# Router products one projection behind their transposes, and the first expert's bias rows asked for before the meeting

## The chip, the cores and the metric

The kernel runs on one core of one Trainium2 chip. The metric is the device time of one execution in microseconds (us). The core has five engines that run their own instruction streams side by side and meet through semaphores: TensorE (PE in the profile), VectorE (DVE), ScalarE (ACT), GpSimd (POOL) and SyncE (SP, which here only asks for transfers). Sixteen DMA engines move data.

## The reference, cut to what matters

One transformer block with a mixture of experts, then a second model of two layers. The change lies in the first block, between the output projection of the mixer and the first expert:

```python
x = x + gate1 * (mixed @ w_out)                      # 512 rows x 1024
h = rmsnorm(x, norm2_w) * (1.0 + scale2) + shift2
logits = h @ w_router + b_router                     # 512 x 32
top_val, top_idx = lax.top_k(logits, 4)
gates = softmax(top_val)
# rows are sorted by expert into blocks of up to 128
hu = xb @ w_up[e] + b_up[e]                          # for each block
act = x_glu * sigmoid(1.702 * x_glu) * (x_lin + 1)
y = act @ w_down[e] + b_down[e]
```

All of this is computed in float32; the bias rows are added as three bfloat16 parts, in a product with ones.

## The kernel before

The kernel is one program in stages. Each stage has one function for each engine (`pe_out1`, `dve_out1`, `act_out1`, `pool_out1` for the router stage; `pe_experts` and so on for the experts), and the code's order in it is the order of that engine's instructions. `meet` joins the engines between stages: each drains and counts up its `finished` semaphore, and each waits for all of them. GpSimd doesn't drain at the meeting ahead of the experts (`but=nc.gpsimd`), but waits for the others.

**Router stage.** The 512 rows are four tiles of 128. `pe_project` (L1286 on) multiplies the mixer's output by `w_out` in two halves of 512 columns (c = 0, 1), each for four tiles: 8 products of 128x512 in float32 make one projection of a tile and a half. In the second half it calls `between(i)` behind tile i's projection. In the kernel before this is `logits(i - 1)`: 4 + 4 transposes of the normed rows of tile i-1 into two PSUM banks (`h2t`, L223), then the product with the router weight, 8 products of 128x32 (L217). The product waits until both banks have been copied into `H2T`: one by VectorE (`features`, L1367), one by ScalarE (L1504). Behind the loop stands `logits(3)`.

VectorE, in `dve_project`, takes each projection out of its bank, multiplies it by the gate (L1308), adds it to x (L1311), and then calls its own `between(i)`: copy half of turned tile i-1 (`features`), make the normed rows of tile i (`h2_rows`, L1356 to L1363, with the sum of squares and the root from ScalarE, L1499 and L1501), and add the bias to the logits of tile i-1 and select its four experts (`logits`, L1371 to L1385, ten small operations in a chain). Behind the loop: `features(3)`, `logits(3)`, and then some 90 small operations that rank the experts and build the row lists.

Each product takes the next of eight PSUM banks in turn (`next_bank`), and waits until the engine that reads that bank has emptied it.

**Meeting and experts.** GpSimd waits for the row lists, gathers the rows of the first two blocks (`pool_gather`, L1682), and waits at the meeting. Then `pool_experts` asks for the bias rows of eight experts (`pool_biases`, L1689), of which the first is always expert 0, in a place known when the kernel is built. TensorE turns the first block's rows (L223), and `pe_up` begins with four products of the bias rows and ones (L1589), which wait for that transfer, before it multiplies by the weights (L1601; L1630 in `pe_down`). Weight tiles of 2 MB come through seven slots; SyncE asks for the next one when TensorE has read the slot's last tile. The expert loads beyond the first expert need VectorE's list of places.

The bias rows of the experts land in `BU`, whose memory the router stage uses for other tiles.

Of the kernel before, what the change touches and what calls it, by code (L numbers as in the profile page):

```python
# [26 lines left out]
NBU = 8  # L27
# [68 lines left out]
def emit(nc, D, out, ctx):  # L96
# [53 lines left out]
    BIASD = dram("bias_rows", (NEXP, 3, 3072), BF16)  # L150
# [9 lines left out]
    done, bank, read = {}, {}, {}  # L160
# [41 lines left out]
    def next_bank(e, key):  # L202
        turn[0] = (turn[0] + 1) % len(order)
        return fill(e, order[turn[0]], key)
# [338 lines left out]
    MIX = alloc(8, 512)  # L543
# [742 lines left out]
    def pe_project(e, src, tcs, tag, between=None):  # L1286

        for c in range(2):
            m, w = take()
            w = x512(w)  # L1290
            e.wait_ge(*landed[m])
            for i in tcs:
                o = next_bank(e, (tag, c, i))
                products(e, o, [(src[:, k, i * 128:i * 128 + 128], w[:, k, :]) for k in range(8)]).then_inc(*pe.up())
                done[tag, c, i] = pe.now()
                if c and between:
                    between(i)
            used[m] = pe.now()
# [15 lines left out]
                    between(i)  # L1314

    def pe_out1(e):
        def logits(i):
            for g in range(2):
                o = next_bank(e, ("h2t", i, g))
                e.wait_ge(*signal("h2_made").at(i + 1))  # L1320
                transposes(e, [(o[:, q * 128:q * 128 + 128], H2[:, i, (4 * g + q) * 128:(4 * g + q + 1) * 128]) for q in range(4)]).then_inc(*pe.up())
                done["h2t", i, g] = pe.now()
            o = next_bank(e, ("logit", i))
            for g in range(2):
                e.wait_ge(*emptied(("h2t", i, g)))
            if i == 0:
                e.wait_ge(*dr.at(96))
            products(e, o[:, 0:32], [(H2T[:, k, i * 128:i * 128 + 128], wr[:, k, :]) for k in range(8)]).then_inc(*pe.up())
            done["logit", i] = pe.now()

        pe_project(e, MIX, range(4), "out1", lambda i: logits(i - 1) if i else None)
        logits(3)
        for l in range(2):
            o = next_bank(e, ("later", l))
            e.wait_ge(*dvr[l].at(16))
            transposes(e, [(o[:, 0:48], vrows2[0:48, l, :])]).then_inc(*pe.up())
            done["later", l] = pe.now()
        o = next_bank(e, "ranks")
        e.wait_ge(*signal("masks").at(1))
        products(e, o[:, 0:128], [(ones, BF[:, 0:4, :]), (U_, MM)])  # L1340
        products(e, o[:, 128:160], [(ones, BF[:, 4, :])]).then_inc(*pe.up())
        done["ranks"] = pe.now()
        o = next_bank(e, "rows")
        for n in range(16):
            u = n % 4
            e.wait_ge(*signal("picks").at(n + 1))
            e.matmul(o[:, 0:NBLK], OP[:, u, :], OBK[:, u, 0:NBLK], start=(n == 0), stop=(n == 15)).then_inc(*pe.up())
            done["pick", n] = pe.now()

    def dve_out1(e):  # L1350
# [14 lines left out]
        def features(i):  # L1365
            e.wait_ge(*done["h2t", i, 0])
            e.tensor_copy(H2T[:, 0:4, i * 128:i * 128 + 128], bank["h2t", i, 0].rearrange("p (k n) -> p k n", n=128)).then_inc(*empties(("h2t", i, 0)))  # L1367
# [28 lines left out]
        def between(i):  # L1396

            if i:
                features(i - 1)
            h2_rows(i)  # L1400
            if i:
                logits(i - 1)

        e.memset(BF[:, 0, :], 0.0).then_inc(*dve.up())
        e.wait_ge(*dr.at(96))
# [1 line left out]
        e.wait_ge(*dg.at(16))  # L1407
        e.wait_ge(*dxa.at(16))
        dve_project(e, range(4), "out1", lambda i: X[:, i, :], lambda i: GR, TM, between)
        features(3)  # L1410
        logits(3)
        for l in range(2):
# [117 lines left out]
    act_out1(nc.scalar)  # L1530
    pool_out1(nc.gpsimd)
    load_on(nc.sync, n_exp + NSLOT)
    row_lists, mix_read = done["row_lists"], done["out1", 1, 3]


    top[0] = base
# [158 lines left out]
    main = Lane("a")  # L1695
# [105 lines left out]
    def pool_experts(e):  # L1801
        places = {}

        def biases(x):
            p = sequence[x]
            xr = in_place(e, places, p)
            rows = BIASD[bass.ds(xr, 1)].rearrange("a k n -> (a k) n") if p else BIASD[0]
            pool_biases(e, main, x, rows, last_block[sequence[x - NBU]] if x >= NBU else None)

        def store(i):  # L1810
            if i < NMAIN - 1:
                pool_store(e, main, i, blocks[i].col)
            for x in range(NBU, NEXP):
                if last_block[sequence[x - NBU]] == i:
                    biases(x)

        for x in range(NBU):
            biases(x)
        for i in range(NMAIN):
            if i + 2 < NMAIN:  # L1820
                pool_gather(e, main, i + 2, blocks[i + 2].col)
            if i and not blocks[i - 1].again:
                store(i - 1)
            if blocks[i].again or i == NMAIN - 1:
                store(i)
# [4 lines left out]
        nc.gpsimd.wait_ge(*t)  # L1830
    for i in range(2):
        pool_gather(nc.gpsimd, main, i, blocks[i].col)
    meet([dz.now()], but=nc.gpsimd)
    next_stage()
    pe_experts(nc.tensor)
# [1061 lines left out]
```

## Time and profile before

| | us |
|---|---|
| median of 3 runs | 2846.61 |
| lowest and highest | 2844.38, 2846.85 |
| the profiled execution | 2849.81 |
| its span in the profile | 2848.6 |
| TensorE busy in it | 2587.0 (91%) |
| VectorE busy | 997.6 (35%) |
| ScalarE busy | 563.5 (20%) |
| GpSimd busy | 170.6 (6%) |
| second half of the output projection to the first expert's start | 573 to 669 |
| expert stage | 669 to 1814 |

Times in the profile are microseconds from the start of the span. The timeline merges like instructions that follow each other; the bracket at the end of a row is the idle time of that engine ahead of it and what ended it. A float32 product is recorded as two instructions, so a projection of 8 products is x16. The granted clock is a share of TensorE's 2.4 GHz; 0.50 is its lower level, 1.2 GHz.

### The profile page before, as it was taken

What the parts mean: (1) busy time and instruction counts of PE and PEld (TensorE: products, weight loads), DVE (VectorE), ACT (ScalarE), POOL (GpSimd) and SP (SyncE); (2) the same over time, 40 slices, a digit from 0 to 9 for tenths busy, and PEclk for the clock granted to TensorE, in tenths of its full rate; (3) what the DMA queues carried; (4) which work ended last, traced back from release to release, by engine and by line L of the source; (5) the groups of instructions that cost most, each with busy time, mean ns of one, the idle gap of its engine ahead of it and who ended that gap; (6) DMA issues with size and microseconds to landing.
All of it is one profiled execution on the core that took longest, in us unless ns stands there. A gap on an engine that the chain in (4) does not pass through costs nothing. (4 is left out here: it accounts for less than half of the span.)

```text
span 2848.6 us, 27020 instructions
## 1 busy us (share of the span) xinstructions
PE 2587.0 (91%) x10285; PEld 1257.0 (44%) x10285; DVE 997.6 (35%) x2141; ACT 563.5 (20%) x1274; POOL 170.6 (6%) x316
## 2 busy tenths in 40 slices
PE   5979788876999999999999999798999889999998
PEld 2534556343434333443443333465544444454453
DVE  2665344353112111111121111435176665332272
ACT  1354313010000000000000000211255443200250
POOL 0000414101000000000000000200000000000000
PEclk8998999987999999999999999899989899999889
DMA  9110175716999999958959999710000002112000
GB/s 327 64 59 30 60 293 166 297 59 260 389 400 416 409 410 415 416 217 338 356 200 370 411 418 416 288 59 26 30 1 1 1 1 82 40 64 89 30 1 30
DMA packets 143354, 565.43 MB, mean 198 GB/s; under 512 B 15429, under 2 KB 36158, under 8 KB 105202
## 3 DMA queue, kind: packets, MB, share of 16 engines
q1 hardware_dynamic: 127336, 515.97, 46.2%
q0 software_dynamic: 12992, 42.51, 4.0%
q10 hardware_dynamic: 2890, 5.13, 0.5%
q8 instruction: 85, 1.39, 0.2%
q14 instruction: 51, 0.42, 0.0%
HBM read 537.24 MB, written 26.35 MB: 198 GB/s over the span
## 5 line engine op out<-in xcount | busy, mean ns | idle before, releaser
L1601 PE MATMUL ps<-ring,mem 128*32 128x512 f32 (+2 forms) x1888 | 517.6, 602 | 8.4 <-issue 8.4
L217 PE MATMUL ps<-mem,ring 128*128 128x512 f32 (+1 forms) x1056 | 421.8, 559 | 2.6 <-DVE mem L737 1.6
L217 PE MATMUL ps<-ring,mem 128*128 128x512 f32 (+5 forms) x1136 | 397.0, 507 | 29.4 <-DVEq L182 15.0
L1601 PEld LDWEIGHTS ps<-ring,mem 128*32 128x32 f32 (+2 forms) x1888 | 189.4, 146 | 276.5 <-issue 276.5
L217 PEld LDWEIGHTS ps<-mem,ring 128*128 128x128 f32 x1056 | 201.5, 192 | 213.2 <-issue 204.6
L217 PEld LDWEIGHTS ps<-ring,mem 128*128 128x128 f32 x1136 | 202.4, 197 | 210.1 <-issue 178.3
L1630 PE MATMUL ps<-ring,mem 128*32 128x512 f32 (+2 forms) x1056 | 273.5, 618 | 11.0 <-issue 11.0
L223 PE MATMUL ps<-mem 128*128 128x128 f32 (+3 forms) x1203 | 195.3, 296 | 70.9 <-DVEq L182 19.8
L1601 PE MATMUL ps<-mem 128*32 128x512 f32 (+2 forms) x800 | 235.0, 596 | 0.0
L223 PEld LDWEIGHTS ps<-mem 128*128 128x128 f32 (+3 forms) x1203 | 146.9, 148 | 195.0 <-issue 126.4
L1662 DVE COPY mem<-ps 128x512 f32<-128x512 f32 x48 | 33.3, 693 | 521.5 <-PE ps L223 521.5
L1670 ACT ACTIVATE mem<-mem 128x512 f32<-128x512 f32 x48 | 28.1, 632 | 771.6 <-DVE mem L1646 771.6
L1638 DVE COPY mem<-ps 128x512 f32<-128x512 f32 x48 | 33.3, 693 | 400.8 <-PE ps L223 400.8
L1630 PEld LDWEIGHTS ps<-ring,mem 128*32 128x32 f32 (+2 forms) x1056 | 100.3, 143 | 161.6 <-issue 161.6
L2350 PE MATMUL ps<-ring 64*128 64x256 f32 (+4 forms) x328 | 132.3, 526 | 14.0 <-ACT mem L2455 4.2
L2405 DVE TENSOR_REDUCE mem<-ps 128x1 f32<-128x768 f32 (+3 forms) x128 | 99.1, 774 | 129.9 <-PE ps L2350 123.0
L1601 PEld LDWEIGHTS ps<-mem 128*32 128x32 f32 (+2 forms) x800 | 83.6, 145 | 107.1 <-issue 107.1
L1630 PE MATMUL ps<-mem 128*128 128x512 f32 (+2 forms) x288 | 119.6, 595 | 0.5 <-issue 0.5
L2465 ACT ACTIVATE ring<-ps 128x768 f32<-128x768 f32 (+2 forms) x128 | 75.5, 603 | 120.9 <-PE ps L223 120.7
L2118 ACT ACTIVATE mem<-ps 128x512 f32<-128x512 f32 (+2 forms) x68 | 33.1, 488 | 331.0 <-PE ps L217 331.0
L2350 PEld LDWEIGHTS ps<-ring 64*128 64x128 f32 (+1 forms) x328 | 62.3, 213 | 62.9 <-issue 49.6
L1677 ACT ACTIVATE mem<-ps 128x512 f32<-128x512 f32 x48 | 26.1, 596 | 310.6 <-PE ps L1630 310.6
(376 smaller groups left out, 2366.7 us busy)
## 6 DMA issues: line engine op xcount, KB each, us to landing
ring<-in_w_up SPq DMA_DIRECT2D x91, 2048.0 KB, 15.7
ring<-in_w_down SPq DMA_DIRECT2D x47, 2048.0 KB, 21.6
mem<-in_w_up SPq DMA_DIRECT2D x37, 2048.0 KB, 19.2
mem<-in_w_down SPq DMA_DIRECT2D x17, 2048.0 KB, 20.7
ring<-in_w_ada SPq DMA_DIRECT2D x12, 2048.0 KB, 7.5
ring<-in_mod_w SPq DMA_DIRECT2D x8, 2048.0 KB, 10.2
ring<-in_cd_w_in SPq DMA_DIRECT2D x6, 2048.0 KB, 7.7
y_rows<-mem POOLq DMA_DIRECT2D x23, 512.0 KB, 8.2
```

What stands on the lines that cost most here:

```text
L217: i = e.matmul(o, l, r, start=(n == 0), stop=(n == len(pairs) - 1))
L223: r = e.transpose(o, i, ident[0:k, 0:k])
L1601: m = e.matmul(PS[n][c0:c0 + rows, :], XGT[:, u, k * 128 + c0:k * 128 + c0 + rows], wt[:, kk, n * 512:n * 512 + 512], start=False, stop=(k ...
L1630: m = e.matmul(PS[6 + n][c0:c0 + rows, :], ACTT[:, k * 128 + c0:k * 128 + c0 + rows], wt[:, kk, n * 512:n * 512 + 512], start=False, stop= ...
L1638: e.tensor_copy(XGT[:, i % 2, hh * 512:hh * 512 + 512], PS[4]).then_inc(L.x_copied, 1)
L1662: e.tensor_copy(ACTT[:, hh * 512:hh * 512 + 512], PS[5]).then_inc(L.a_copied, 1)
L1670: e.activation(SG[:, c], T1[:, c], ACT.Sigmoid, scale=1.702).then_inc(L.gate, 1)
L1677: e.activation(Y[:, i % 2, n * 512:n * 512 + 512], PS[6 + n], ACT.Copy).then_inc(L.y_copied, 1)
L2118: e.activation(dst, bank[key][:, 0:n], func).then_inc(*empties(key))
L2350: m = e.matmul(PP[x % 2][:, at:at + k.shape[1]], q, k, start=True, stop=True)
L2405: e.tensor_reduce(m[:, 0:1], PP[x % 2][:, lo:lo + n], AX.X, ALU.max).then_inc(*dve.up())
L2465: m = e.activation(A.groups[g][1][a][:, to:to + k1 - k0, c * 128:c * 128 + 128], PP[2][:, k0 * 128:k1 * 128].rearrange("p (k n) -> p k n", ...
```

## The change

Router stage, TensorE: the function `logits` is split. `turn_h2(i)` does the transposes of tile i, `logits(i)` the product. Behind the projection of tile i TensorE now does `turn_h2(i - 1)` and then `logits(i - 2)`; behind the loop `logits(2)`, `turn_h2(3)`, `logits(3)`. VectorE's `between(i)` keeps the copy of turned tile i-1 and the normed rows of tile i, and selects for tile i-2 rather than i-1; behind the loop it selects for tile 2, copies turned tile 3, and selects for tile 3. ScalarE's code is the same.

Meeting: GpSimd asks for expert 0's bias rows behind the two gathers and ahead of the meeting. A wait stands in front of it, for the product of tile 3, since the rows go to memory that the router's products read. `pool_experts` begins with the second expert of its sequence.

```diff
--- before.py
+++ after.py
@@ -1314,12 +1314,14 @@
                     between(i)
 
     def pe_out1(e):
-        def logits(i):
+        def turn_h2(i):
             for g in range(2):
                 o = next_bank(e, ("h2t", i, g))
                 e.wait_ge(*signal("h2_made").at(i + 1))
                 transposes(e, [(o[:, q * 128:q * 128 + 128], H2[:, i, (4 * g + q) * 128:(4 * g + q + 1) * 128]) for q in range(4)]).then_inc(*pe.up())
                 done["h2t", i, g] = pe.now()
+
+        def logits(i):
             o = next_bank(e, ("logit", i))
             for g in range(2):
                 e.wait_ge(*emptied(("h2t", i, g)))
@@ -1328,7 +1330,16 @@
             products(e, o[:, 0:32], [(H2T[:, k, i * 128:i * 128 + 128], wr[:, k, :]) for k in range(8)]).then_inc(*pe.up())
             done["logit", i] = pe.now()
 
-        pe_project(e, MIX, range(4), "out1", lambda i: logits(i - 1) if i else None)
+        def between(i):
+
+            if i:
+                turn_h2(i - 1)
+            if i > 1:
+                logits(i - 2)
+
+        pe_project(e, MIX, range(4), "out1", between)
+        logits(2)
+        turn_h2(3)
         logits(3)
         for l in range(2):
             o = next_bank(e, ("later", l))
@@ -1398,8 +1409,8 @@
             if i:
                 features(i - 1)
             h2_rows(i)
-            if i:
-                logits(i - 1)
+            if i > 1:
+                logits(i - 2)
 
         e.memset(BF[:, 0, :], 0.0).then_inc(*dve.up())
         e.wait_ge(*dr.at(96))
@@ -1407,6 +1418,7 @@
         e.wait_ge(*dg.at(16))
         e.wait_ge(*dxa.at(16))
         dve_project(e, range(4), "out1", lambda i: X[:, i, :], lambda i: GR, TM, between)
+        logits(2)
         features(3)
         logits(3)
         for l in range(2):
@@ -1530,7 +1542,7 @@
     act_out1(nc.scalar)
     pool_out1(nc.gpsimd)
     load_on(nc.sync, n_exp + NSLOT)
-    row_lists, mix_read = done["row_lists"], done["out1", 1, 3]
+    row_lists, mix_read, features_read = done["row_lists"], done["out1", 1, 3], done["logit", 3]
 
 
     top[0] = base
@@ -1814,7 +1826,7 @@
                 if last_block[sequence[x - NBU]] == i:
                     biases(x)
 
-        for x in range(NBU):
+        for x in range(1, NBU):
             biases(x)
         for i in range(NMAIN):
             if i + 2 < NMAIN:
@@ -1830,6 +1842,9 @@
         nc.gpsimd.wait_ge(*t)
     for i in range(2):
         pool_gather(nc.gpsimd, main, i, blocks[i].col)
+    assert sequence[0] == 0
+    nc.gpsimd.wait_ge(*features_read)
+    pool_biases(nc.gpsimd, main, 0, BIASD[0], None)
     meet([dz.now()], but=nc.gpsimd)
     next_stage()
     pe_experts(nc.tensor)
```

TensorE's order in the second half of the output projection, before. x48 is the first half and two tiles of the second; L223 x8 are the transposes of a tile; 128x32 are the router's products.

```order
L217 MATMUL ps<-ring,mem 128x512 x48
L223 MATMUL ps<-mem 128x128 x8
L217 MATMUL ps<-mem 128x32 x8
L217 MATMUL ps<-ring,mem 128x512 x8
L223 MATMUL ps<-mem 128x128 x8
L217 MATMUL ps<-mem 128x32 x8
L217 MATMUL ps<-ring,mem 128x512 x8
L223 MATMUL ps<-mem 128x128 x8
L217 MATMUL ps<-mem 128x32 x8
L223 MATMUL ps<-mem 128x128 x8
L217 MATMUL ps<-mem 128x32 x8
```

The same place on TensorE with the change:

```order
L217 MATMUL ps<-ring,mem 128x512 x48
L223 MATMUL ps<-mem 128x128 x8
L217 MATMUL ps<-ring,mem 128x512 x8
L223 MATMUL ps<-mem 128x128 x8
L217 MATMUL ps<-mem 128x32 x8
L217 MATMUL ps<-ring,mem 128x512 x8
L223 MATMUL ps<-mem 128x128 x8
L217 MATMUL ps<-mem 128x32 x16
L223 MATMUL ps<-mem 128x128 x8
L217 MATMUL ps<-mem 128x32 x8
```

The products of tiles 0 and 1 stand one projection later, the one of tile 1 now behind the last projection, in a row with that of tile 2.

GpSimd around the meeting, before, with the semaphores that each instruction waits for. L1682 are the gathers, L1689 the bias rows, L380 reads an expert's number; the `finished` semaphores are the meeting.

```order
L1524 DMA h_rows<-mem 128x1024 [waits h2_made] x4
L1682 DMA mem<-h_rows,mem 128x1024 [waits dma_h2,bank_free1,pe_step]
L1682 DMA mem<-h_rows,mem 128x1024
L1689 DMA mem<-bias_rows 3x3072 [waits pool_finished,act_finished,dma_zero,dve_finished,pe_finished]
L380 TENSOR_LOAD mem [waits dve_step]
L380 ISA x2
L1689 ISA
L1689 DMA mem<-bias_rows 3x3072
```

The same place on GpSimd with the change (`pe_step` on the bias rows is the product of tile 3):

```order
L1536 DMA h_rows<-mem 128x1024 [waits h2_made] x4
L1694 DMA mem<-h_rows,mem 128x1024 [waits dma_h2,bank_free1,pe_step]
L1694 DMA mem<-h_rows,mem 128x1024
L1701 DMA mem<-bias_rows 3x3072 [waits pe_step]
L380 TENSOR_LOAD mem [waits pool_finished,dma_zero,act_finished,dve_step,dve_finished,pe_finished]
L380 ISA x2
L1701 ISA
L1701 DMA mem<-bias_rows 3x3072
```

The first request for bias rows has left the meeting's waits to the instruction behind it.

## Rows read from the trace of the kernel before

**Rows 1.** Timeline, TensorE, router and first expert (start, us, engine line operation, idle before)
```profile
587.51 1.04 PE L223 MATMUL ps<-mem 128*128 128x128 f32 x8
591.48 1.94 PE L217 MATMUL ps<-mem 128*128 128x32 f32 x16 [2.93 <-ACT mem L1504]
593.26 8.81 PE L217 MATMUL ps<-ring,mem 128*128 128x512 f32 x16
...
605.82 2.38 PE L217 MATMUL ps<-mem 128*128 128x32 f32 x16 [2.88 <-ACT mem L1504]
608.02 8.37 PE L217 MATMUL ps<-ring,mem 128*128 128x512 f32 x16
616.22 1.04 PE L223 MATMUL ps<-mem 128*128 128x128 f32 x8
620.14 2.99 PE L217 MATMUL ps<-mem 128*128 128x32 f32 x16 [2.88 <-ACT mem L1504]
...
626.54 3.59 PE L217 MATMUL ps<-mem 128*128 128x32 f32 x16 [1.66 <-DVE mem L1367]
...
661.96 1.09 PE L223 MATMUL ps<-mem 128*128 128x128 f32 x4 [7.21 <-DVEq L182]
664.02 1.09 PE L223 MATMUL ps<-mem 128*128 128x128 f32 x4 [0.97 <-DVE mem L1638]
669.22 1.88 PE L1589 MATMUL ps<-mem 3*128 3x512 bf16 x4 [4.11 <-DMA mem<-bias_rows]
```

**Rows 2.** Timeline, VectorE, router
```profile
592.29 1.23 DVE L1363 TENSOR_TENSOR mem<-mem 128x1024 f32<-128x1024 f32 x1
...
621.05 1.23 DVE L1363 TENSOR_TENSOR mem<-mem 128x1024 f32<-128x1024 f32 x1
623.16 0.19 DVE L1371 TENSOR_TENSOR mem<-ps,mem 128x32 f32<-128x32 f32 x1 [0.88 <-PE ps L217]
...
625.75 0.69 DVE L1367 COPY mem<-ps 128x512 f32<-128x512 f32 x1
630.17 0.19 DVE L1371 TENSOR_TENSOR mem<-ps,mem 128x32 f32<-128x32 f32 x1 [3.73 <-PE ps L217]
```

**Rows 3.** Timeline, GpSimd, second gather and first request for bias rows
```profile
657.59 0.97 POOL L1682 DMA_INDIRECT mem<-h_rows,mem  x1 [0.31 <-issue]
662.42 0.58 POOL L1689 DMA_DIRECT2D mem<-bias_rows  x1 [3.86 <-DVE mem L1491]
```

**Rows 4.** Timeline, TensorE, transposes and projections in a later stage
```profile
2454.23 1.04 PE L223 MATMUL ps<-mem,ring 128*128 128x128 f32 x8
2455.10 7.03 PE L217 MATMUL ps<-ring,mem 128*128 128x512 f32 x16
```

**Rows 5.** Windows: length, busy time (instructions) of PE, PEld, DVE, ACT, POOL, clock, DMA share, GB/s
```profile
593.00:596.00 3.00, 3.00 (x8) 1.46 (x8) 2.72 (x14) 0.00 (x0) 0.54 (x1) 0.58 0.37 150
...
626.00:629.00 3.00, 2.46 (x12) 2.48 (x12) 0.44 (x1) 0.82 (x1) 0.00 (x0) 0.50 0.01 3
671.00:674.00 3.00, 3.00 (x5) 1.42 (x5) 0.00 (x0) 0.00 (x0) 1.30 (x2) 0.50 1.02 405
674.00:677.00 3.00, 3.00 (x6) 1.19 (x6) 0.00 (x0) 0.00 (x0) 0.00 (x0) 0.76 1.01 386
710.00:713.00 3.00, 3.00 (x18) 1.00 (x16) 0.00 (x0) 0.00 (x0) 0.00 (x0) 1.00 0.02 5
```

**Rows 6.** DMA: second gather, first bias request (us to landing), all bias-row transfers
```profile
mem<-h_rows,mem POOLq DMA_INDIRECT x1, 4.9
...
mem<-bias_rows POOLq DMA_DIRECT2D x1, 18.0 KB, 6.7
...
DMA to landing us min/median/max: 2.5/7.8/10.0
```

**Rows 7.** Waits of TensorE, expert stage, 660 to 1760 us (in total, times, longest)
```profile
PE ps L1601 <- issue: 8.4, 5, 3.6
...
PE ps L1630 <- issue: 3.9, 2, 3.1
```


## The prediction

> **What bounds the kernel now.** I read the waits of the router stage first, then its TensorE and VectorE timelines, then the windows of the expert stage. The question is not which engine is busiest over 2848.6 us, but which wait ends last in the two places that the change touches, and whether what is won there arrives at the end.
>
> *Router.* In the second half of the output projection TensorE does, for each tile i after the first: project tile i, turn the normed rows of tile i-1 (8 transposes), multiply them by the router weight. The product needs both copies of the turned tile out of PSUM, so TensorE stands still behind the transposes: 2.93 us before the product of tile 0, and 2.88 before that of tile 1 [rows 1]. The third such gap, before the product of tile 2, comes after the last projection. From the last projection on VectorE leads: it makes the normed rows of tile 3, selects for tile 2, copies half of turned tile 3, waits for the product of tile 3, selects for tile 3 (630.17), and goes on in one chain of small dependent operations to 661.8, which releases TensorE at 661.96 [rows 1, 2]. So the stage ends when tile 3's logits exist plus a constant, and those hang on when the last projection ends.
>
> *Meeting.* TensorE turns the first block's rows and is ready at 664.02 + 1.09 = 665.11. It starts the first expert at 669.22, after 4.11 us of waiting for the bias rows, which GpSimd asks for at 662.42, just behind the meeting [rows 1, 3].
>
> **Part 1, projections ahead of products.** The transposes of tile i-1 are now followed at once by projection i+1, and the product of i-1 stands one projection later. I build TensorE's new order from starts. The same alternation of 8 transposes and a projection runs elsewhere at the full clock: 0.87 us from the start of the transposes to that of the projection, which is recorded at 7.03 [rows 4] and overlaps what follows by some 0.16 (608.02 + 8.37 is 0.17 past 616.22, [rows 1]), so 6.87 to the next transposes. The product takes 593.26 - 591.48 = 1.78 from start to start [rows 1].
> - Turn tile 0 at 587.51 (unchanged), projection 2 at 588.38, turn tile 1 at 595.25, product 0 at 596.12, projection 3 at 597.90, turn tile 2 at 604.77. Before, turn tile 2 began at 616.22 [rows 1]. So it is **11.45 us** earlier: two gaps of 2.93 and 2.88; the product of tile 1, 608.02 - 605.82 = 2.20, now behind; two projections at 7.03 in place of 8.81 and 8.37, that is 3.12; and 0.3 of overlap.
> - The 3.12 need an argument. Projection 2 ran with a granted clock of 0.58 in 593 to 596, between the levels 1.2 and 2.4 GHz, though its predecessor ran full: the clock fell after 5.7 us in which TensorE had only transposes, a gap and the short product [rows 1, 5]. With the gap filled the clock should hold, as it does in the alternation of rows 4; the difference is the product of 32 columns that now stands beside the transposes.
> - Is the input ready? Turn tile 1 needs the normed rows of tile 1, whose last step ends at 592.29 + 1.23 = 593.52 [rows 2]: 1.7 us before 595.25. Product 0's copies (late by 2.9 us behind the transposes before) have a whole projection to finish in. PSUM banks rotate over eight and the order of TensorE's takes and of the copies leaves none late.
>
> **Part 1, what stands behind the last projection.** Before, VectorE's normed rows of tile 3 were ready at 621.05 + 1.23 = 622.28 [rows 2], 6.06 us after the start of turn tile 2 (616.22). That delay is VectorE's and ScalarE's own and stays: 604.77 + 6.06 = 610.83. Behind it VectorE now has two selections, of tiles 1 and 2, where it had one. One takes 625.75 - 623.16 = 2.59 [rows 2]. So 610.83 + 2 x 2.59 = 616.01 for the start of the copy of half of turned tile 3; from that copy to the product 626.54 - 625.75 = 0.79, and from the product to the selection of tile 3 630.17 - 626.54 = 3.63 [rows 1, 2]: 616.01 + 0.79 + 3.63 = 620.43 against 630.17. **The router is 9.7 us shorter**; 1.7 of the 11.45 go to the second selection (2.59, less the 0.88 that VectorE used to wait for product 2). TensorE fits in beside it: product 2 came 3.92 us after the start of turn tile 2 (620.14), so now at about 608.7, and tile 3 is turned by 613, with 3 us to spare.
>
> The 3.63 are a product at the low level, clock 0.50 in 626 to 629 [rows 5]. TensorE again has 3 us idle ahead of it, so I keep them. At the full level it would be 1.94, as product 0 [rows 1]: at best 1.7 more.
>
> All that follows (the chain of VectorE, the lists, the meeting, the first load of a chosen expert, which waits for VectorE's list) moves with 630.17, so these 9.7 us arrive whole.
>
> **Part 2, the bias rows.** GpSimd asks for expert 0's rows right behind its two gathers. Its new wait, for the product of tile 3, was met some 30 us earlier, and nothing queues behind it that it could hold. The second gather is issued at 657.59 for 0.97 us [rows 3], so the request goes out near 658.7 (in the old time) rather than 662.42, 3.7 us earlier. It landed 6.7 us after issue [rows 6]: 665.4. TensorE starts at 665.4 instead of 669.22: **3.8 us**. Bounds: all 4.1 if it lands before 665.1. At the other end its slowest landing of the whole trace, 10.0 us [rows 6], gives 668.7 and 0.5. I take 6.7, measured for this very request with three large transfers beside it; the gather's 4.9 [rows 6] means that the queue ahead is empty at 662.5, so nothing long is in the way. GpSimd's other bias requests follow the meeting in the old order, one place sooner.
>
> The Trainium skill, "DMA: Bandwidth & Descriptors", section "Queues, rings and completion order", says that a completion lands only after every earlier write of the same DMA engine, over all queues. By that rule the request now has only the gathers ahead of it and not the weight and context loads of 660 to 663, and the 6.7 would shrink; landing near 663, it would give 4.1 and a sum 0.3 larger. No row of before shows the request in that place.
>
> **Does the stage of the experts keep it?** It could be that the weight stream sets its pace. In 660 to 1760 TensorE waits 8.4 + 3.9 us for transfers [rows 7], so the stream is near its limit. But in 710 to 713 the DMA engines are 0.02 busy [rows 5]: they have caught up and wait for TensorE to free a slot, so the stream restarts from TensorE's time and takes its shift along. Before that, loads are asked for well ahead of their use. I take nothing off.
>
> **Sum.** 9.7 + 3.8 = 13.5 us. The profiled execution took 2849.81 us and would take 2836.3; the median of the runs is 3.2 lower, 2846.61, and would become **2833.1 us**, 0.47% less.
>
> **Rivals.**
> - *The clock falls in projections 2 and 3 all the same.* Speaks for it: turn and product together are 3 us of light work, and the clock fell after such work before, with a gap in it. Against: rows 4, and no gap remains. Price: the 3.12, so 10.4 us and 2836.2. The Trainium skill, "TensorE: Matmul & The Clock Gate", section "What's actually happening", puts the clock down to a monitor of recent activity that runs free of the kernel; by it the moment of a fall is partly luck, which lends this rival its chance.
> - *The bias rows bring little.* The small request lands late (10.0 us), or the load stream beside it takes back what TensorE wins: the slots of expert 0 come free earlier while the engines are 1.02 busy in 671 to 674 [rows 5]. Then only the router counts, 9.7 to 10.2 us: 2836.7. The change then does half of what it says.
> - *More than forecast.* The clock, low until about 675 [rows 5], rises sooner because TensorE is busy without a gap from 661.96: half of the 4.1 us moved, 2.0; product 3 at the full level, 1.7; bias 4.1. Sum 17.5, 2829.1.
> - *Slower: the weight stream slips.* Place: the waits of the expert products for landed tiles [rows 7]. An earlier TensorE meets the stream where it cannot follow, and each wait is followed by a stretch at the low clock: from 671 to 675 such a stretch cost about 2 us. If seven waits double (12.3 us) and each brings one more such stretch (up to 14), 26 us come against 13.5: 2846.6 - 13.5 + 26 = 2859. It decides from 13.5 us given back, and shows as slower from 19.2. Half of it, 7.8 to 19.2, would show as no change. Against: the idle DMA engines at 710, from which both start together.
>
> **How the numbers follow.** Forecast (2831.5 to 2835) 60 in 100; clock falls 13; bias brings little 11; more than forecast 7; stream slips 9, of which 6 end within 0.2% and 3 slower. Within 0.2% (5.7 us, about what a measurement of this kernel can tell from no change): 6; faster by more: 91; slower: 3. The range leaves out the stream rival and runs from 2829.1, less 1 us for the runs, to 2839.8, where the clock falls and the bias brings 0.5 (9.7 - 3.1 + 0.5 = 7.1, so 2839.5): 2828 to 2840.
>
> **What would show it.** Right: no gap between the transposes and projection 2 or 3, both at 7.0 us; from the start of turn tile 0 to that of turn tile 2 17.3 us; from there to the selection of tile 3 15.7 us (13.95 before); bias rows asked for within 0.5 us of the second gather, and under 0.5 us of wait before the first expert; waits for tiles in the expert stage near 12 us in sum. Wrong: projections over 8 us; a wait of 2 us or more for the bias rows; a stage of experts, from its first bias product to the start of the next stage, longer by some us than before.

## The result, and the profile after

| | before | changed |
|---|---|---|
| median, 6 runs each (us) | 2847.22 | 2833.23 |
| lowest, highest | 2844.38, 2856.25 | 2827.69, 2836.06 |
| the profiled execution | 2849.81 | 2832.91 |
| its span | 2848.6 | 2831.7 |

The ratio is 0.9941, with a 95% interval from 0.9924 to 0.9959: 0.4 to 0.8% faster. The medians differ by 14.0 us and the profiled executions by 16.9.

TensorE in the router stage of the changed kernel, and up to the first expert (the timeline: start, us, engine, line, operation, idle time before it and what ended it). It answers to [rows 1]:

```profile
587.69 1.04 PE L223 MATMUL ps<-mem 128*128 128x128 f32 x8
588.57 7.03 PE L217 MATMUL ps<-ring,mem 128*128 128x512 f32 x16
595.43 1.04 PE L223 MATMUL ps<-mem 128*128 128x128 f32 x8
596.31 1.87 PE L217 MATMUL ps<-mem 128*128 128x32 f32 x16
598.01 7.11 PE L217 MATMUL ps<-ring,mem 128*128 128x512 f32 x16
604.96 1.04 PE L223 MATMUL ps<-mem 128*128 128x128 f32 x8
...
608.88 1.94 PE L217 MATMUL ps<-mem 128*128 128x32 f32 x16 [1.17 <-ACT mem L1516]
...
616.90 3.60 PE L217 MATMUL ps<-mem 128*128 128x32 f32 x16 [3.80 <-DVE mem L1378]
...
652.33 1.09 PE L223 MATMUL ps<-mem 128*128 128x128 f32 x4 [7.21 <-DVEq L182]
654.39 1.08 PE L223 MATMUL ps<-mem 128*128 128x128 f32 x4 [0.98 <-DVE mem L1650]
655.40 1.88 PE L1601 MATMUL ps<-mem 3*128 3x512 bf16 x4
657.22 23.22 PE L1613 MATMUL ps<-ring,mem 128*128 128x512 f32 x48
```

No row from 587.69 to 604.96 has a bracket: both gaps of 2.9 us are gone, and both projections take 7.0 to 7.1 us where they took 8.81 and 8.37. The bias product at 655.40 has no bracket either; it waited 4.11 us before. The wait that grew is the one ahead of the product of tile 3, 3.80 us (1.66 before).

VectorE behind the last projection, for [rows 2]: the end of the normed rows of tile 3, the selections of tiles 1 and 2, the copy of half of turned tile 3, the selection of tile 3.

```profile
609.79 1.23 DVE L1374 TENSOR_TENSOR mem<-mem 128x1024 f32<-128x1024 f32 x1
610.93 0.18 DVE L1382 TENSOR_TENSOR mem<-ps,mem 128x32 f32<-128x32 f32 x1
...
613.52 0.19 DVE L1382 TENSOR_TENSOR mem<-ps,mem 128x32 f32<-128x32 f32 x1
...
616.11 0.69 DVE L1378 COPY mem<-ps 128x512 f32<-128x512 f32 x1
620.54 0.19 DVE L1382 TENSOR_TENSOR mem<-ps,mem 128x32 f32<-128x32 f32 x1 [3.73 <-PE ps L217]
```

GpSimd at the meeting, for [rows 3]. The first request for bias rows goes out with the second gather, the next one behind the meeting:

```profile
647.95 0.97 POOL L1694 DMA_INDIRECT mem<-h_rows,mem  x1 [0.31 <-issue]
648.92 0.60 POOL L1701 DMA_DIRECT2D mem<-bias_rows  x1
653.83 0.55 POOL L1701 DMA_DIRECT2D mem<-bias_rows  x1 [4.31 <-issue]
```

Windows of the changed kernel (length, busy times and counts of PE, PEld, DVE, ACT, POOL, then granted clock, DMA share, GB/s), for [rows 5]. The clock stays at 1.00 through the router's projections and falls behind the last one:

```profile
593.00:596.00 3.00, 3.00 (x13) 1.51 (x12) 1.06 (x2) 0.00 (x0) 0.54 (x1) 1.00 0.29 117
...
605.00:608.00 3.00, 2.71 (x25) 2.59 (x23) 2.13 (x4) 1.15 (x2) 0.00 (x0) 1.00 0.00 0
611.00:614.00 3.00, 1.94 (x8) 1.57 (x8) 2.62 (x17) 0.84 (x2) 0.53 (x1) 0.50 0.43 175
```

TensorE's waits for transfers from 660 to 1760 us, for [rows 7]: 14.4 us in sum, 12.3 before. These fixed limits cut the two executions at different places, since the changed one is 14 us ahead at their far end. Counted over the whole stage, from the first bias product to the stage behind the experts, the waits are 11.6 + 8.4 = 20.0 us before and 11.4 + 9.6 = 21.0 in the changed kernel.

```profile
PE ps L1613 <- issue: 9.6, 6, 3.3
...
PE ps L1642 <- issue: 4.8, 3, 3.2
```

The stage behind the experts starts with this row (14.01 us earlier than before, where it is 1814.39):

```profile
1800.38 1.94 PE L223 MATMUL ps<-mem 128*128 128x128 f32 x8 [10.14 <-PEq L1950]
```

### The profile page after: what moved, and what is told of

Same layout as the page of the kernel before. It is cut to its first block and busy times, and to the rows that moved or that the text cites. A ratio compares the mean times of both kernels' runs of the same rounds, so it can differ in the third digit from the quotient of the medians.

```text
span 2831.7 us, 27022 instructions
## 1 busy us (share of the span) xinstructions
PE 2577.2 (91%) x10285; PEld 1254.2 (44%) x10285; DVE 997.4 (35%) x2141; ACT 563.0 (20%) x1274; POOL 170.3 (6%) x316
## 5 line engine op out<-in xcount | busy, mean ns | idle before, releaser
L217 PE MATMUL ps<-ring,mem 128*128 128x512 f32 (+5 forms) x1136 | 390.8, 501 | 29.9 <-DVEq L182 15.0
L1642 PE MATMUL ps<-ring,mem 128*32 128x512 f32 (+2 forms) x1056 | 268.0, 598 | 11.4 <-issue 11.4
L223 PE MATMUL ps<-mem 128*128 128x128 f32 (+3 forms) x1203 | 195.6, 297 | 72.5 <-DVEq L182 19.9
L223 PEld LDWEIGHTS ps<-mem 128*128 128x128 f32 (+3 forms) x1203 | 147.0, 149 | 196.7 <-issue 129.1
L1682 ACT ACTIVATE mem<-mem 128x512 f32<-128x512 f32 x48 | 28.1, 632 | 771.9 <-DVE mem L1658 771.9
L1689 ACT ACTIVATE mem<-ps 128x512 f32<-128x512 f32 x48 | 26.1, 596 | 305.0 <-PE ps L1642 305.0
```

What stands on the lines that cost most here:

```text
L217: i = e.matmul(o, l, r, start=(n == 0), stop=(n == len(pairs) - 1))
L223: r = e.transpose(o, i, ident[0:k, 0:k])
L1642: m = e.matmul(PS[6 + n][c0:c0 + rows, :], ACTT[:, k * 128 + c0:k * 128 + c0 + rows], wt[:, kk, n * 512:n * 512 + 512], start=False, stop= ...
L1682: e.activation(SG[:, c], T1[:, c], ACT.Sigmoid, scale=1.702).then_inc(L.gate, 1)
```

## The experiments

Executions reach the router up to 7 us apart, and the later stages differ from one execution to the next by more than the change is worth (below). So the traces are compared by stretches between fixed places. A is from the turn of tile 0 on TensorE to the selection of tile 3 on VectorE. B is from there to the first bias product. C is from there to the first transposes of the stage behind the experts. All are differences of starts in the timelines, in us.

| kernel | A | B | C | ratio to before, interval |
|---|---|---|---|---|
| before | 42.66 | 39.05 | 1145.2 | |
| changed | 32.85 | 34.86 | 1145.0 | 0.9941, 0.9924 to 0.9959 |
| e1_router | 32.85 | 38.98 | 1146.4 | 0.9969, 0.9952 to 0.9985 |
| e2_bias | 42.66 | 34.88 | 1145.9 | 0.9990, 0.9978 to 1.0002 |
| e3_fill | 39.08 | 38.34 | 1145.4 | 0.9989, 0.9972 to 1.0006 |
| e4_tail | 30.34 | 34.88 | 1143.1 | 0.9937, 0.9915 to 0.9959 |
| e5_warm | 32.85 | 33.96 | 1145.7 | 0.9958, 0.9944 to 0.9971 |
| e6_after | 32.85 | 34.88 | 1145.2 | 0.9951, 0.9937 to 0.9966 |
| e7_both | 30.33 | 34.19 | 1145.1 | 0.9933, 0.9919 to 0.9946 |
| e8_mark | 32.85 | 34.89 | 1146.7 | |
| e9_hold | 29.02 | 34.87 | 1145.4 | 0.9933, 0.9915 to 0.9951 |
| e10_all | 29.02 | 33.68 | 1142.1 | 0.9930, 0.9913 to 0.9947 |
| e11_tail2 | 30.33 | 34.86 | 1143.9 | 0.9947, 0.9931 to 0.9963 |

A repeats within 0.03 us for the same code, and so does B in the kernels that ask early for the bias rows (34.86 to 34.89), so a tenth of a microsecond in these can be read. B is less certain where its end is a wait for the bias rows: from the selection of tile 3 on, the kernel before, e1_router and e3_fill have the same code, and B is 39.05, 38.98 and 38.34. Absolute starts that an expectation names hold for a router that starts as in the kernel before; the differences are what can be compared.

**One part alone: e1_router and e2_bias.** Against the changed kernel, e1_router asks for the bias rows where the kernel before did:

```diff
-    nc.gpsimd.wait_ge(*features_read)
-    pool_biases(nc.gpsimd, main, 0, BIASD[0], None)
     meet([dz.now()], but=nc.gpsimd)
...
-        for x in range(1, NBU):
+        for x in range(NBU):
```

e2_bias is the kernel before with these lines the other way round.

> Only part 1: the products one projection behind their transposes; GpSimd asks for the first bias rows behind the meeting, as in the kernel before. My theory: the selection of tile 3 starts 9.7 us earlier than in the kernel before (630.17 us of its span becomes 620.5), TensorE still waits about 4.1 us for the bias rows, and the first bias product starts at 659.4 instead of 669.22; the next stage (first transposes at 1814.4 before) starts at 1804.7; the whole is 9.7 us shorter, ratio 0.9966. Rival (the two parts are not additive, since an earlier meeting changes what stands beside the bias transfer): the bias wait is above 5 or under 3 us, and the gain at the first expert is off 9.7 by the same. Second rival (the weight stream takes gains back): the gain at the start of the next stage is smaller than at the first expert by 2 us or more.

> Only part 2: the first bias rows asked for ahead of the meeting; the router stage as before. The trace of the changed kernel showed no wait at all for the bias rows. My theory: the wait of 4.11 us before the first bias product goes and nothing takes its place, so that product starts at 665.1 instead of 669.22, and the stage behind the experts starts 4.1 us earlier (1810.3); ratio 0.9986. Rival (the weight stream takes it back, because the loads of chosen experts are asked for at the same time as before and TensorE only reaches them sooner): the gain at the start of the next stage is under 2 us and the waits of the expert products for transfers, 12.3 us before, grow by the rest. This is the sharper place to see it than the whole change, since here TensorE moves and the start of the stream does not.

e1_router, the first expert on TensorE:

```profile
663.28 1.88 PE L1601 MATMUL ps<-mem 3*128 3x512 bf16 x4 [4.03 <-DMA mem<-bias_rows]
```

e2_bias, the same place:

```profile
661.75 1.09 PE L223 MATMUL ps<-mem 128*128 128x128 f32 x4 [0.97 <-DVE mem L1638]
662.77 1.88 PE L1589 MATMUL ps<-mem 3*128 3x512 bf16 x4
```

Part 1 alone takes 9.81 us off A and leaves B; part 2 alone leaves A and takes 4.17 off B. The wait of 4.03 us is there with part 1 alone, so an earlier meeting hardly changes it; in e3_fill below, where only the router's order of work differs, it is 3.40, so the wait itself varies by some 0.7 us. The parts add: 9.81 + 4.19 in the changed kernel. Against the B of e3_fill, part 2 would be worth 3.5. C changes by +1.2, +0.7 and -0.2 us in the three; the same code gives 1145.0 and 1145.2 in two executions, 1143.1 and 1143.9 in two others (e4_tail, e11_tail2), and e8_mark, whose instructions before the experts differ only on GpSimd, 1146.7. No loss of 2 us or more in the weight stream shows; one of up to some 1.5 us cannot be told from that scatter. The waits for transfers over the whole stage are 19.9 us in e2_bias against 20.0 before, so they did not take back what part 2 won. By whole times e1_router's ratio is clear of 1 and fits 0.9966; e2_bias at 0.9990 is 2.8 us, inside an interval that just reaches 1, so its 4.2 us are read from the trace.

**What made the clock fall: e3_fill.** The order of before, with work put into the two gaps:

```diff
             o = next_bank(e, ("logit", i))
+            for n in range(6 if i < 2 else 0):
+                transposes(e, [(o[:, q * 128:q * 128 + 128], H2[:, i, q * 128:q * 128 + 128]) for q in range(4)])
             for g in range(2):
                 e.wait_ge(*emptied(("h2t", i, g)))
```

> The kernel before, with its order, but in the two gaps behind the transposes of tiles 0 and 1 TensorE does 24 more transposes of the same rows into the bank of the product that follows (2.6 us of work in gaps of 2.93 and 2.88; nobody reads them). Theory (the idle gap makes the clock fall): the granted clock stays at 1.0 through projections 2 and 3, they take 7.0 us instead of 8.81 and 8.37, and the selection of tile 3 comes about 3.1 us earlier; 3.1 us off the whole. Rival (light work is what makes it fall, transposes and a product of 32 columns as much as a gap): the clock falls as before, the projections keep 8.4 to 8.8 us, gain 0, or a loss of some tenths where the transposes run past the gap.

e3_fill on TensorE, transposes (x32 now), product and projection:

```profile
588.20 3.66 PE L223 MATMUL ps<-mem 128*128 128x128 f32 x32
592.02 1.94 PE L217 MATMUL ps<-mem 128*128 128x32 f32 x16 [0.17 <-issue]
593.80 7.11 PE L217 MATMUL ps<-ring,mem 128*128 128x512 f32 x16
...
606.45 7.11 PE L217 MATMUL ps<-ring,mem 128*128 128x512 f32 x16
```

Useless transposes in the gaps, and projection 2 takes 7.11 instead of 8.81, projection 3 7.11 instead of 8.37. A is 3.58 us shorter: 2.96 in the projections, 0.4 in the product of tile 1, and small rests. So 5.6 us of transposes and small products with hardly any idle time did not make the clock fall, and the same stretch with 2.9 us of idle time in it did. The rival of the prediction, that light work is what lowers it, is out for this place. Nor is it chance: all ten traces with the new order show the two projections at 7.03 and 7.11, and both traces with the old order and empty gaps (before, e2_bias) show them at 8.81 and at 8.37 or 8.40. The Trainium skill, "TensorE: Matmul & The Clock Gate", section "What's actually happening", has the clock follow a monitor of TensorE's own recent activity; e3_fill, where nothing but TensorE's activity in the gaps was changed, agrees. The run also measures the clock's share of part 1 by itself: about 3 us of the 9.8 are the clock, the others idle time and order. Its whole time (0.9989) fits the 3.1 us that were expected but is not clear of 1, so this too is read from the trace.

**What the order costs behind the last projection: e4_tail.** One swap on VectorE, on the changed kernel:

```diff
-        logits(2)
         features(3)
+        logits(2)
         logits(3)
```

> The changed kernel, with one swap on VectorE behind the last projection: the copy of half of turned tile 3 stands ahead of the selection of tile 2, no longer behind it. In the changed kernel product 3 started at 616.90, behind two selections (5.1 us) and the copy. Theory (the second selection on the path is what part 1 costs): the copy ends at 614.2, product 3 starts near 614.3, the selection of tile 2 (2.57 us) runs beside it, the selection of tile 3 starts at 617.9 instead of 620.54; 2.6 us less than the changed kernel, 16.4 us less than the kernel before by the places up to the experts, ratio 0.9942. Rival: the copy has to wait for the transposes of tile 3 (they end at 613.1), and the selections of VectorE bound the end, so that under 1.5 us are won.

e4_tail, the product of tile 3 on TensorE, and the selection behind it on VectorE:

```profile
614.78 3.60 PE L217 MATMUL ps<-mem 128*128 128x32 f32 x16 [1.21 <-DVE mem L1378]
```

```profile
613.99 0.69 DVE L1378 COPY mem<-ps 128x512 f32<-128x512 f32 x1
618.49 0.19 DVE L1382 TENSOR_TENSOR mem<-ps,mem 128x32 f32<-128x32 f32 x1 [1.34 <-PE ps L217]
```

A is 30.34, 2.51 us less. So the second selection did stand on the path, as the prediction's tail term had it, and it need not: a copy that TensorE waits for belongs ahead of work that nobody waits for. The product of tile 3 still took 3.60 us at the low clock.

**Holding the clock there: e9_hold.** e4_tail, and transposes that nobody reads in the two gaps behind the last projection (`filler` does four into the bank o as many times as its second argument says):

```diff
             o = next_bank(e, ("logit", i))
+            if i >= 2:
+                filler(o, 3 if i == 2 else 4, i)
             for g in range(2):
```

> e4_tail with filling transposes (nobody reads them) in the two gaps behind the last projection: 12 ahead of the product of tile 2 (1.3 us in a gap of 1.2), 16 ahead of that of tile 3 (1.75 us in a gap of 1.2 to 2). In e4_tail the clock fell to 0.50 at about 611 and the product of tile 3 took 3.60 us. Theory (idle time, not light work, makes the clock fall; e3_fill showed it in the gaps ahead of projections 2 and 3): the clock stays at 1.0 up to the product of tile 3, which takes 1.9 us, and from the turn of tile 0 to the selection of tile 3 it is 28.7 us instead of 30.34. Rival (without any dense product for some microseconds the clock falls whatever stands in the gaps): 30.3 us again, product of tile 3 3.6 us.

e9_hold, TensorE:

```profile
607.80 1.50 PE L223 MATMUL ps<-mem 128*128 128x128 f32 x12
609.14 1.94 PE L217 MATMUL ps<-mem 128*128 128x32 f32 x16
611.43 2.81 PE L223 MATMUL ps<-mem 128*128 128x128 f32 x24 [0.35 <-DVE mem L1380]
614.53 1.97 PE L217 MATMUL ps<-mem 128*128 128x32 f32 x16 [0.29 <-DVE mem L1384]
```

The product takes 1.97 us instead of 3.60 and A is 29.02, 1.32 less. 0.3 of the 1.6 are not won, since VectorE's selection of tile 2 now ends last (616.93; the product ends at 616.50).

**The clock at the first expert: e5_warm, e7_both, e10_all.** TensorE is idle for 7.2 us ahead of the meeting, and the first expert starts at the low clock in every kernel so far. e5_warm adds, behind the products of the row lists:

```diff
+        e.wait_ge(*emptied(("logit", 2)))
+        for n in range(4):
+            e.matmul(bank["logit", 2].rearrange("p (a n) -> p a n", n=128), ident, ones.unsqueeze(1).to_broadcast([128, 4, 128]), start=True, stop=True)
```

> The changed kernel, with four more products of 128x512 (float32, the identity by ones, nobody reads them) on TensorE between the last product of the row lists and the meeting ahead of the experts, where it is idle for 7.2 us. In the changed kernel the first expert's products run at a granted clock of 0.50 from 655.4 to about 662. Theory (the low stretch is the price of the idle time ahead of the experts): the four products take 6.8 us at the low level and end before VectorE does, the meeting is not later, and the clock is at 1.0 some 6 us earlier, so the 48 instructions behind the first bias products take about 20.6 us instead of 23.22; 2.5 to 3.3 us less than the changed kernel from the first bias product on. Rival (the two short gaps at the meeting, 1 us each, undo it, or products of ones and zeros don't raise the clock): the 48 instructions keep 22.7 to 23.5 us, gain 0.

e5_warm, TensorE, and two windows:

```profile
645.48 5.34 PE L1362 MATMUL ps<-mem 128*128 128x512 f32 x8
652.89 0.63 PE L223 MATMUL ps<-mem 128*128 128x128 f32 x4 [2.07 <-DVEq L182]
654.49 0.63 PE L223 MATMUL ps<-mem 128*128 128x128 f32 x4 [0.97 <-DVE mem L1653]
655.05 1.33 PE L1604 MATMUL ps<-mem 3*128 3x512 bf16 x4
656.32 23.92 PE L1616 MATMUL ps<-ring,mem 128*128 128x512 f32 x48
```

```profile
650.00:653.00 3.00, 0.93 (x3) 0.14 (x2) 2.59 (x11) 0.00 (x0) 0.08 (x1) 1.00 0.99 299
...
656.00:659.00 3.00, 3.00 (x4) 1.18 (x4) 0.00 (x0) 0.00 (x0) 1.15 (x4) 0.50 1.01 421
```

My theory failed here. The clock did rise ahead of the meeting (the turns take 0.63 instead of 1.09, and B is 0.9 shorter), and fell again behind it: the 48 instructions take 23.92, longer than the 23.22 of the changed kernel, and nothing is left. The four products ended 2.07 us early, and the turns have a gap of 0.97. e7_both has the swap of e4_tail and these four products.

> The swap of e4_tail and the four products of e5_warm together, on the changed kernel. If both act in their own place they add: 2.5 us less from the turn of tile 0 to the selection of tile 3, and the 48 instructions behind the first bias products near 20.6 us; some 5 us less than the changed kernel, 19 less than the kernel before, ratio 0.993. Where e5_warm brings nothing, this is e4_tail again, ratio 0.994.

A is 30.33 as in e4_tail, and B 34.19, 0.7 shorter; behind the bias products 23.09 us. It is e4_tail with little more. e10_all is e9_hold with the gaps nearly closed: six products instead of four, and behind the first turn

```diff
         pe_turn_x(e, main, 0, 0)
+        transposes(e, [(PS[5][:, q * 128:q * 128 + 128], ones) for q in range(4)])
+        transposes(e, [(PS[5][:, q * 128:q * 128 + 128], ones) for q in range(4)])
         pe_turn_x(e, main, 0, 1)
```

> e9_hold, with six products of 128x512 ahead of the meeting (four in e5_warm, which ended 2.1 us before VectorE did) and 8 filling transposes between the two turns of the first block (gap 0.97 us). In e5_warm the clock rose to 1.0 ahead of the meeting and fell to 0.50 behind it, in the first expert's first products. Theory (the gaps at the meeting made it fall): with the gaps nearly closed it stays at 1.0, and from the first bias product to the end of the 48 instructions behind it it takes 21.5 us (0.8 and 20.7) instead of 25.0 in the changed kernel; 3 us less. Rival (the transposes and the bias products are too light to hold it, or the picks of 128x41 products, which ran at 0.50 though TensorE was busy through, count for nothing): it falls again, 24 us or more from the first bias product on. No later than e9_hold by more than 0.3 us either way at the meeting.

e10_all, TensorE, and a window:

```profile
652.11 2.23 PE L223 MATMUL ps<-mem 128*128 128x128 f32 x16 [0.65 <-DVEq L182]
654.27 1.04 PE L1610 MATMUL ps<-mem 3*128 3x512 bf16 x4
655.24 20.87 PE L1622 MATMUL ps<-ring,mem 128*128 128x512 f32 x48
```

```profile
656.00:659.00 3.00, 3.00 (x8) 1.33 (x7) 0.00 (x0) 0.00 (x0) 1.49 (x3) 1.00 0.98 365
```

From the first bias product to the end of the 48 instructions it is 655.24 + 20.87 - 654.27 = 21.84, against 657.22 + 23.22 - 655.40 = 25.04 in the changed kernel: 3.2 us, and B is 1.2 shorter. The clock is 1.00 where it was 0.50. Three things differ at once from e5_warm: more dense products, a shorter wait behind them (0.65 us for 2.07), and transposes in the gap between the turns. This one trace does not say which of them held the clock. From the turn of tile 0 to the stage behind the experts e10_all takes 1204.7 us, the changed kernel 1212.7, the kernel before 1226.9. In whole times it is 2828.14 at the median, ratio 0.9930; its interval still overlaps that of the changed kernel, and the median of e9_hold beside it is 2828.95, so the 3.2 us are shown by the trace alone.

**When the bias rows land: e8_mark.**

```diff
     pool_biases(nc.gpsimd, main, 0, BIASD[0], None)
+    nc.gpsimd.wait_ge(main.biased[0], 16)
     meet([dz.now()], but=nc.gpsimd)
```

> The changed kernel, in which GpSimd also waits for the landing of the first bias rows right behind its request, so that its next instruction shows when they landed; nobody waits for GpSimd at this meeting. The prediction took 6.7 us from issue to landing, as the request behind the meeting needed, which would have left TensorE waiting for 0.3 us; it did not wait. Theory (the transfer is short where the weight and context loads are not ahead of it, and has only the gather ahead): it lands 3 to 5 us after issue, and before the weight load that follows the list of places. Rival (6 to 7 us is what such a request takes in any company): 6 us or more, and TensorE was only just not late.

e8_mark, GpSimd:

```profile
652.11 0.97 POOL L1694 DMA_INDIRECT mem<-h_rows,mem  x1 [0.30 <-issue]
653.09 0.60 POOL L1701 DMA_DIRECT2D mem<-bias_rows  x1
659.41 0.55 POOL L1701 DMA_DIRECT2D mem<-bias_rows  x1 [5.72 <-issue]
```

In the changed kernel TensorE resumes behind the meeting at 652.33, and the second request comes 1.5 us later, at 653.83. Here TensorE resumes at 656.49, so without a late landing the request would come at 658.0; it comes at 659.41. Taken back by the same 1.5, the landing was seen at about 657.9, 4.8 us after issue. That is worked out, not read: the trace records no landing for this request (5.7 us is that of the next one). TensorE, whose bias product starts at 659.58, had about 1.7 us to spare. A bound can be read in other runs. In e10_all the request goes out at 648.71 and the bias product starts at 654.27 without a wait, so the rows had landed after 5.6 us at most; in e5_warm the same holds from 649.48 to 655.05. The rival of 6 us or more in any company is out. Behind the meeting the same request took 6.7 us (before), and TensorE's waits put it at about 6.6 in e1_router and 6.0 in e3_fill. The second gather, asked for at 652.11, landed after 5.3, at 657.4, so the small request lands just behind the one ahead of it. The rule of the Trainium skill, "DMA: Bandwidth & Descriptors", section "Queues, rings and completion order", that a completion lands only after the earlier writes of its DMA engine, is in agreement with that and with a landing sooner than 6.7, though no run here parts it from plain order in one queue.

**The later stages: e6_after and e11_tail2.** e6_after is the changed kernel again, e11_tail2 is e4_tail again.

> The changed kernel once more. It is there for the later stages, which the change does not touch: from the first transposes of the stage behind the experts to the last stretches of the attention stages the executions so far took either 637.4 to 637.5 us or 630.9 to 632.0 between the same two waits (the one of 3.88 us for ScalarE's queue, the one of 3.73 us for GpSimd's), the kernel before and the changed one both 637.4. Theory (the clock there falls or holds by the moment, whatever the kernel): the time between these waits is one of the two again, not bound to the kernel, while the router (32.85 us from the turn of tile 0 to the selection of tile 3) and the way from there to the first bias product (34.86) repeat within 0.1. Rival (the change has moved the later stages for good): 637.4 again, here and in every kernel with part 1 and part 2.

> e4_tail once more, beside e9_hold and e10_all on one chip. The places of the change repeat within 0.1 us: 30.34 us from the turn of tile 0 to the selection of tile 3, 34.88 from there to the first bias product. In the attention stages, between the wait of 3.88 us for ScalarE's queue and that of 3.73 us for GpSimd's, e4_tail, e7_both and e2_bias took 631 to 632 us, the seven other executions 637.4. Theory (by the moment): either value may come. Rival (a kernel has its value for good): 632 again.

The two waits named there, in e4_tail and then in e11_tail2, which are the same code:

```profile
2030.19 4.52 PE L2365 MATMUL ps<-ring 64*128 64x512 f32 x8 [3.90 <-ACTq L182]
...
2662.17 3.75 PE L2365 MATMUL ps<-ring 64*128 64x256 f32 x8 [3.74 <-POOLq L182]
```

```profile
2032.88 4.73 PE L2365 MATMUL ps<-ring 64*128 64x512 f32 x8 [3.88 <-ACTq L182]
...
2670.27 2.57 PE L2365 MATMUL ps<-ring 64*128 64x256 f32 x8 [3.72 <-POOLq L182]
```

632.0 us in the one and 637.4 in the other. The difference is not bound to a kernel. The whole time spreads accordingly: 12 runs of e1_router lie between 2828.31 and 2846.11. e6_after gave 637.4 again, which the theory also allowed, so e11_tail2 settles it. By whole times the small steps from one of these kernels to the next can't be told apart: e4_tail and e11_tail2 have medians of 2825.59 and 2832.37.

## Why the prediction was right

The time on record was 2833.1 and the median is 2833.2. The mechanisms are the ones forecast; that the two times agree to 0.1 us is luck (last point). Point by point:

- **The order on TensorE.** 17.3 us were forecast from the turn of tile 0 to that of tile 2; 604.96 - 587.69 = 17.27. The clock held, as the alternation of [rows 4] suggested, and e3_fill shows the reason: the idle gap, not the light work, had lowered it.
- **Behind the last projection.** 15.7 us were forecast to the selection of tile 3; 620.54 - 604.96 = 15.58. Two selections stood on the path, e4_tail takes one off and wins the 2.5. The product of tile 3 ran at the low clock, 3.60. The router gained 9.81 where 9.7 was forecast.
- **The bias rows.** Forecast was 3.8 us, measured 4.19. The mis-sized term is the landing: 6.7 us were taken over from a request that stood behind the meeting, where three large transfers were asked for beside it; in its new place it took 5.6 us at most (e10_all), by the estimate of e8_mark 4.8, and nobody waited. The 4.1 that the prediction worked out beside the rule of the Trainium skill ("DMA: Bandwidth & Descriptors", section "Queues, rings and completion order") was closer than the 3.8, but the 0.3 between them is less than the 0.7 by which the old wait varies. That the company of the request makes the difference is argued, not shown: no run changed it alone.
- **The expert stage.** "I take nothing off" held: C is 1145.2 and 1145.0, and the sum at the stage behind the experts is 14.0 us, 9.81 + 4.19 less 0.2 for a later start of the router and plus 0.2 in C. The waits for transfers were to stay near 12 us and were 14.4 in the same limits, but about half of the difference is where the limits fall: over the whole stage they are 20.0 and 21.0, while TensorE's busy time there fell from 1104.9 to 1101.4. No run says which of the two follows from the change.
- **The whole.** The profiled executions differ by 16.9, not 13.5. Of the remaining 2.9, 2.75 lie between 1814.39 and 2050.15, in a stage that the change does not touch: the mean clock over it was 0.95 in the execution of before and 0.97 in the changed one. Eight instructions alone, behind the same wait of 2.08 us, took 4.54 us before and 2.85 in the changed kernel. That part is of the same kind as the scatter above and is no gain of the change. The agreement of the time on record with the median to 0.1 us is luck, since neither is known that well: the medians of six runs moved by 14.0, while the ratio of 0.9941 stands for 16.8 and that of the repeat (e6_after), 0.9951, for 13.9.
- **The sums.** Two slips change nothing: the range names 2839.8 where its own terms give 2839.5, and the request for bias rows would go out at 658.56 by [rows 3], not 658.7.

## What to carry to other kernels

When one engine's product waits for another engine's copy, put the next independent dense product between them: the gap goes, and with it the low clock that the gap brings to what follows. Once the loop is staggered so, look at the drain: what the staggering has pushed behind the last step must not stand ahead of the copy that the last product needs. And take the latency of a moved transfer from a request in the same company, or hold both ends.

## What the runs showed of the hardware

- **Idle time lowered TensorE's clock in the router, light work didn't.** With 3.66 us of transposes in place of 1.04 and a gap of 2.93, the projection behind the next product took 7.11 us instead of 8.81 (e3_fill). At the meeting four dense products raised the clock to 1.00, and after 2.07 and 0.97 us without work it was at 0.50 again (e5_warm); with six products, 0.65 us without work and the second gap filled it stayed (e10_all). Work that nobody reads gave 3.2 us there.
- **The same instructions need not meet the fall at the same moment.** Behind the last projection the product of tile 2 follows an idle gap of 1.17 us in the changed kernel and in e1_router, with the same TensorE code ahead of it, and takes 1.94 us in the one and 3.08 in the other (3.10 in e8_mark). The product of tile 3, 3.6 us in each, and A are not touched by it.
- **Outside of the change, the clock makes the whole time of this kernel scatter by several microseconds.** The same 504 matrix instructions of the attention stages took 151.60 us in the execution of before and 143.50 in that of e2_bias, which has the same code there, at a granted clock of 0.89 and 0.95. The kernel before, and then e2_bias:

```profile
2176.95:2328.55 151.60, 128.82 (x504) 67.33 (x504) 99.30 (x265) 78.22 (x164) 1.71 (x6) 0.89 0.00 1
```

```profile
2171.04:2314.54 143.50, 119.56 (x504) 62.11 (x504) 99.30 (x265) 77.81 (x164) 1.98 (x6) 0.95 0.00 1
```

What decides between the two stays open: e4_tail and e11_tail2 are the same code and differ. A change of 0.2% in this kernel is therefore better read from stretches of the trace than from whole times.
